# Nine input loads and three constants moved from the head of the filter stage's DMA queue to places between its stores

## The chip, the cores and the metric

One NeuronCore of one Trainium2 chip. The metric is the device time of one execution in microseconds, median of three runs.

## What is computed

One encoder layer over 2048 tokens of 1024 channels (batch 1). Cut to what matters here:

```
mod = silu(c) @ w_ada + b_ada ; shift, scale, gate = split(mod, 3)
u = x * (1 + scale) + shift
proj = u @ w_in + b_in                       # 1024 -> 3072 channels, all 2048 tokens
h = sin(...) of position features            # small network, three layers
k = (h @ w_out_filter) * decay ; k_freq = rfft([k forward, k backward], n = 4096)   # two filters x 512 channels
z = v ; for o, g in (x1, x2): z = g * (irfft(rfft(z) * k_freq[o]) + bias[o] * z)
y = concat(z * silu(gate_h), pooled branch * silu(gate_p))
out = LayerNorm(alpha * x + gate * (y @ w_out + b_out)) * ln_g + ln_b
```

## The kernel before, in words

The Fourier transforms are done as two stages of matrix products with a trip through HBM between them. Every fp32 product is three products of split operands (a "high" part, written by ScalarE, and a "low" part, the rest, written by VectorE). The program is a row of blocks with an all-engine barrier between some of them:

1. `front`: the small network, and the sums for `scale1` and `shift`. Its SP queue ends with the store of two gate rows (L357).
2. `filter_stage1` (scope `fs1`, L490 to L610): the filters are generated and go through the first transform stage. This is the stage that is changed.
3. `values_and_filters` (scope `p1`): the rest of the filters' transform, the forming and splitting of `u`, and the first tiles of the input projection.
4. Four more blocks, of the same kind as to queues, up to the output.

`filter_stage1` has N = 32 units, numbered n, two for each of 16 token groups m. For each unit:

- TensorE `gen(n)`: six matmuls into `gen_ps` (L538; the first two units have two more, L541).
- VectorE `window(n)`: times the decay, into `fs_k` (L570).
- ScalarE `high(n)`: `fs_khi` (L593). VectorE `low(n)`, one unit behind its window: `fs_klo` (L578).
- TensorE `stage1(n)`, three units behind `gen`: twelve matmuls into `s1_ps` (L554), with a table of 256 KB for each two units. The tables are loaded ahead on the GpSimd queue into a ring of three (L291).
- ScalarE `evac(n)`, three units behind `high`: copies `s1_ps` into one of three 512 KB buffers `xo[n % 3]` (L598). It waits for `stored[n % 3]`, that is, until the store of unit n - 3 has landed.
- SP: waits for `evac(n)` and stores the buffer to `kseq` in HBM, 512 KB (L516).

ScalarE takes its work in the order high(n), step(n - 2), evac(n - 3); `step` is empty but for unit 29, where it splits the first projection weight (`w_high(0)`, L761). VectorE ends the stage with `w_low(0)` and `form_u` of input pieces 0 to 3 (L720). TensorE runs gen(n), then stage1(n - 3); `stage1(n)` waits for `evac(n - 2)`.

The three `xo` buffers lie in memory that the projection owns and uses later (two thirds of `row`, half of `cv`); the eight buffers of `load_x` are `xin_xt` (two), `side`, the other half of `cv`, and `xin_pair` (four). Which piece goes to which:

```
def load_x(self, sp, m):
    tc, k2 = m // 4, m % 4
    src = self.t["t_xt"].rearrange("(k p) c -> p k c", p=P)
    after(sp, self.ulo_done[m % 8], m // 8)
    sp.dma_start(self.xt[m % 8][:, :, :], src[:, 2 * k2:2 * k2 + 2, tc * CH:(tc + 1) * CH]).then_inc(self.xt_in[m % 8], 16)
```

A piece is 512 KB in runs of 2 KB. Pieces 0 to 3 are first read by `form_u` at the end of the stage, pieces 4 to 7 in the next block. `load_w(sp, 0)` (L754) is 512 KB, first read by `w_high(0)`. `load_consts` (L746 to L748) are three small transfers, 38, 32 and 64 KB, first read in the next block.

Of the kernel before, what the change touches and what calls it, by code (L numbers as in the profile page):

```python
# [487 lines left out]
def group_rows(seq, g):  # L488

    return seq.rearrange("(p m g) c -> p g m c", m=2, g=GS)[:, g, :, :]  # L490


def filter_stage1(nc, t, tabs, fl, kseq, pj, owner):


    with Scope(nc, "fs1", cleared_with=owner) as s:
# [9 lines left out]
        N = 2 * GS  # L506

        @block.sync
        def _(sp):
            for m in range(8):  # L510
                pj.load_x(sp, m)
            pj.load_w(sp, 0)
            pj.load_consts(sp)
            for n in range(N):
                sp.wait_ge(evac_done[n % 2], n // 2 + 1)
                sp.dma_start(group_rows(kseq[n % 2], fl.group(n // 2)), xo[n % 3]).then_inc(stored[n % 3], 16)  # L516
            sp.wait_ge(fl.rows_out, 16)

        @block.gpsimd
# [1885 lines left out]
```

## Time and profile before

| | |
|---|---|
| median of 3 runs | 1191.55 us (1189.43 to 1192.32) |
| the profiled execution | 1192.32 us, span 1190.4 us |
| TensorE busy, share of the span | 92% |
| VectorE, ScalarE, GpSimd | 72%, 48%, 1% |
| HBM traffic | 273.24 MB, mean 230 GB/s |
| granted TensorE clock, mean | 0.971 of full |

The span is 1.9 us shorter than the execution's own time, since it begins with the first recorded instruction and ends with the last. Start times in the profile count from the span's start. Busy shares are means over stages with different limits, so the stage that is changed has to be read by itself: `filter_stage1` lies at 55 to 140 us.

### The profile page before, as it was taken

What the parts mean: (1) busy time and instruction counts of PE and PEld (TensorE: products, weight loads), DVE (VectorE), ACT (ScalarE), POOL (GpSimd) and SP (SyncE); (2) the same over time, 40 slices, a digit from 0 to 9 for tenths busy, and PEclk for the clock granted to TensorE, in tenths of its full rate; (3) what the DMA queues carried; (4) which work ended last, traced back from release to release, by engine and by line L of the source; (5) the groups of instructions that cost most, each with busy time, mean ns of one, the idle gap of its engine ahead of it and who ended that gap; (6) DMA issues with size and microseconds to landing.
All of it is one profiled execution on the core that took longest, in us unless ns stands there. A gap on an engine that the chain in (4) does not pass through costs nothing. (4 is left out here: it accounts for less than half of the span.)

```text
span 1190.4 us, 14193 instructions
## 1 busy us (share of the span) xinstructions
PE 1089.8 (92%) x4928; PEld 840.9 (71%) x4928; DVE 856.6 (72%) x1093; ACT 576.8 (48%) x757; POOL 12.6 (1%) x32
## 2 busy tenths in 40 slices
PE   3799789999999999989999998897999578999995
PEld 1278667888888777767888776665788467888883
DVE  6699976555454546559999555655999857888878
ACT  4078864434545344537777443442877753222210
POOL 0001000000000000000000000000000000000000
PEclk8789999999999999999999999999999889999998
DMA  9998845677674536688998578778899999557321
GB/s 338 350 310 285 288 164 162 195 249 248 217 254 161 176 109 213 229 253 240 275 297 258 160 235 268 232 254 212 245 298 261 306 308 311 156 184 211 125 89 54
DMA packets 155133, 273.24 MB, mean 230 GB/s; under 512 B 11504, under 2 KB 49520, under 8 KB 153397
## 3 DMA queue, kind: packets, MB, share of 16 engines
q1 hardware_dynamic: 151605, 266.74, 70.2%
q0 software_dynamic: 3168, 5.51, 2.0%
q8 instruction: 40, 0.66, 0.3%
q14 instruction: 32, 0.25, 0.1%
q10 hardware_dynamic: 288, 0.08, 0.0%
HBM read 178.95 MB, written 98.57 MB: 233 GB/s over the span
## 5 line engine op out<-in xcount | busy, mean ns | idle before, releaser
L177 PE MATMUL u_pp<-uh_uhi,prj_whi 128*128 128x512 f32 x768 | 310.3, 404 | 14.6 <-DVE u_ulo L741 9.1
L178 PE MATMUL u_pp<-u_ulo,prj_whi 128*128 128x512 f32 x768 | 305.2, 397 | 0.0
L179 PE MATMUL u_pp<-uh_uhi,prj_wlo 128*128 128x512 f32 x768 | 305.0, 397 | 0.0
L177 PEld LDWEIGHTS u_pp<-uh_uhi,prj_whi 128*128 128x128 f32 x768 | 146.0, 190 | 57.9 <-issue 14.9
L179 PEld LDWEIGHTS u_pp<-uh_uhi,prj_wlo 128*128 128x128 f32 x768 | 146.1, 190 | 34.6
L178 PEld LDWEIGHTS u_pp<-u_ulo,prj_whi 128*128 128x128 f32 x768 | 146.5, 191 | 32.3
L1256 DVE TENSOR_TENSOR p_alo<-xin_pair,p_ahi 128x1024 fp32r<-128x1024 f32 x32 | 39.2, 1226 | 100.8 <-ACT p_ahi L1193 100.8
L1193 ACT ACTIVATE p_ahi<-xin_pair 128x1024 fp32r<-128x1024 f32 x32 | 33.9, 1061 | 126.8 <-PE p_ps L179 119.0
L2195 ACT ACTIVATE p_sm<-p_mv,p_eps 128x1 f32<-128x1 f32 x16 | 4.7, 295 | 107.8 <-DVE p_mv L2286 107.8
L177 PE MATMUL p_first<-uh_uhi,prj_whi 128*128 128x512 f32 x128 | 51.5, 403 | 4.0 <-DVE p_y L2280 2.6
L593 ACT ACTIVATE fs_khi<-fs_k 128x1024 fp32r<-128x1024 f32 x32 | 34.0, 1061 | 41.2 <-DVE fs_k L570 41.2
L554 PE MATMUL fs_s<-fs_khi,flt_tab 64*128 64x512 f32 x256 | 50.1, 413 | 3.3 <-ACT prj_row L598 3.3
L1595 ACT ACTIVATE p_us<-p_u 64x512 f32<-64x512 f32 x64 | 38.1, 596 | 27.7 <-DVE p_y L1672 26.6
L178 PE MATMUL p_first<-uh_uhi,prj_whi 128*128 128x512 f32 x128 | 51.1, 399 | 0.0
L179 PE MATMUL p_first<-uh_uhi,prj_wlo 128*128 128x512 f32 x128 | 51.0, 399 | 0.0
L177 PE MATMUL p_b<-uh_uhi,prj_whi 128*128 128x512 f32 x128 | 50.6, 395 | 0.2 <-DVE p_us L2280 0.2
L179 PE MATMUL p_b<-uh_uhi,prj_wlo 128*128 128x512 f32 x128 | 50.5, 395 | 0.0
L178 PE MATMUL p_b<-uh_uhi,prj_whi 128*128 128x512 f32 x128 | 50.5, 395 | 0.0
L1678 DVE TENSOR_TENSOR p_us<-p_us,p_k_im 128x512 f32<-128x512 f32 x64 | 43.4, 688 | 9.4 <-ACT p_us L1596 6.2
L797 ACT ACTIVATE prj_row<-u_pp,prj_own 128x512 f32<-128x512 f32 x64 | 43.9, 687 | 6.6 <-PE u_pp L179 5.7
L900 ACT ACTIVATE prj_side<-u_pp,prj_own 128x512 f32<-128x512 f32 x32 | 38.9, 1216 | 13.2 <-PE u_pp L179 7.5
L570 DVE TENSOR_TENSOR fs_k<-fs_gen,flt_dec 128x1024 f32<-128x1024 f32 x32 | 38.8, 1212 | 7.7 <-PE fs_gen L541 7.7
(210 smaller groups left out, 2108.0 us busy)
## 6 DMA issues: line engine op xcount, KB each, us to landing
xin_pair<-kseq SPq DMA_DIRECT2D x32, 512.0 KB, 4.4
kfreq<-xin_pair SPq DMA_DIRECT2D x32, 512.0 KB, 5.2
xseq<-p_xo SPq DMA_DIRECT2D x32, 512.0 KB, 7.5
p_k_re<-kfreq SPq DMA_DIRECT2D x64, 256.0 KB, 5.5
p_k_im<-kfreq SPq DMA_DIRECT2D x64, 256.0 KB, 4.8
bseq<-p_out SPq DMA_DIRECT2D x32, 512.0 KB, 5.3
prj_ws<-in_t_win SPq DMA_DIRECT2D x24, 512.0 KB
kseq<-prj_row SPq DMA_DIRECT2D x22, 512.0 KB, 4.3
```

The costliest lines, as they stand in the source:

```text
L177: nc.tensor.matmul(out, w[0], m[0], start=start, stop=False, skip_group_check=True)
L178: nc.tensor.matmul(out, w[0], m[1], start=False, stop=False, skip_group_check=True)
L179: return nc.tensor.matmul(out, w[1], m[0], start=False, stop=stop, skip_group_check=True)
L554: mm = nc.tensor.matmul(s1_ps[r][:, jj, :], fl.tab[m % 3][js, h, a, :], k[r3][js, h, :], start=h == 0 and part == 0, stop=h == 1 and part ...
L570: nc.vector.tensor_tensor(kf[r3][:, :, :], gen_ps[n % 2][:, :, :], fl.dec[:, m // 2, :, :], ALU.mult).then_inc(k_done[r3], 1)
L593: nc.scalar.activation(khi[r3][:, :, :], kf[r3][:, :, :], ACT.Copy).then_inc(hi_done[r3], 1)
L797: self.nc.scalar.activation(self.row[:, PAD + c * CH:PAD + (c + 1) * CH], self.pp[q % 2][:, :], ACT.Identity, bias=self.b_in[:, col:col + ...
L900: self.nc.scalar.activation(by_group(self.sg[:, c % 2, :]), by_token(self.pj.pp[q % 2][:, :]), ACT.Silu, bias=self.pj.b_in[:, col:col + 1] ...
L1193: nc.scalar.activation(ahi[:, :, :], a[n % 2][:, :, :], ACT.Copy).then_inc(hi_done, 1)
L1256: nc.vector.tensor_tensor(alo[:, :, :], a[n % 2][:, :, :], f32(ahi[:, :, :]), ALU.subtract).then_inc(lo_done, 1)
L1595: nc.scalar.activation(us[0:64, i, :], u_ps[64:128, i, :], ACT.Copy, scale=-1.0)
L1678: nc.vector.tensor_tensor(us[:, i, :], us[:, i, :], k_im[:, i, :], ALU.mult).then_inc(turn_done, 1)
```

## The change

The nine loads and the constants are taken from the head of the SP queue of `filter_stage1` and issued behind stores of late units: the weight behind the store of unit 18, pieces 0 to 3 behind those of units 19 to 22, the constants behind unit 23, pieces 4 to 7 behind units 24 to 27. Nothing else differs: same transfers, same sizes, same buffers, same waits.

```diff
@@ -507,13 +507,17 @@
         @block.sync
         def _(sp):
-            for m in range(8):
-                pj.load_x(sp, m)
-            pj.load_w(sp, 0)
-            pj.load_consts(sp)
             for n in range(N):
                 sp.wait_ge(evac_done[n % 2], n // 2 + 1)
                 sp.dma_start(group_rows(kseq[n % 2], fl.group(n // 2)), xo[n % 3]).then_inc(stored[n % 3], 16)
+                if n == N - 14:
+                    pj.load_w(sp, 0)
+                if N - 13 <= n < N - 9:
+                    pj.load_x(sp, n - (N - 13))
+                if n == N - 9:
+                    pj.load_consts(sp)
+                if N - 8 <= n < N - 4:
+                    pj.load_x(sp, n - (N - 12))
             sp.wait_ge(fl.rows_out, 16)
```

## Rows read from the trace of the kernel before

**Rows 1.** Busy time by stretch; last three columns: TensorE clock, DMA share, GB/s.

```profile
core 0: us, PE busy (x) PEld busy (x) DVE busy (x) ACT busy (x) POOL busy (x), PEclk, DMA share, GB/s
55.00:70.00 15.00, 14.57 (x62) 8.49 (x64) 8.54 (x8) 4.69 (x5) 0.00 (x0) 0.59 1.01 373
70.00:80.00 10.00, 9.99 (x81) 7.86 (x79) 10.00 (x10) 8.54 (x10) 1.59 (x3) 1.00 0.78 259
...
120.00:130.00 10.00, 10.00 (x88) 8.93 (x86) 10.00 (x10) 8.83 (x10) 1.07 (x2) 1.00 0.95 315
```

**Rows 2.** Same view, stretches of 2 us: loads alone, then stores and tables.

```profile
66.00:68.00 2.00, 2.00 (x16) 1.62 (x14) 2.00 (x3) 1.06 (x1) 0.00 (x0) 0.70 1.05 396
...
70.00:72.00 2.00, 1.99 (x18) 1.50 (x16) 2.00 (x3) 1.71 (x3) 0.54 (x1) 1.00 0.34 45
78.00:80.00 2.00, 2.00 (x19) 1.61 (x17) 2.00 (x3) 1.71 (x3) 0.53 (x1) 1.00 1.05 408
```

**Rows 3.** ScalarE's timeline: start, duration, what; in brackets its idle time before.

```profile
70.74 1.06 ACT L593 ACTIVATE fs_khi<-fs_k 128x1024 fp32r<-128x1024 f32 x1 [0.29 <-DVE fs_k L570]
71.71 1.01 ACT L598 ACTIVATE prj_row<-fs_s 128x1024 f32<-128x1024 f32 x1
...
130.65 1.00 ACT L598 ACTIVATE prj_row<-fs_s 128x1024 f32<-128x1024 f32 x1
...
133.85 1.00 ACT L598 ACTIVATE prj_row<-fs_s 128x1024 f32<-128x1024 f32 x1
...
138.10 1.03 ACT L598 ACTIVATE prj_row<-fs_s 128x1024 f32<-128x1024 f32 x1 [0.38 <-PE fs_s L554]
```

**Rows 4.** Timeline of the SP queue, 69 to 140 us; x2 rows hold two stores.

```profile
70.48 2.82 SPq L516 DMA_DIRECT2D kseq<-prj_row  x2
...
111.27 2.78 SPq L516 DMA_DIRECT2D kseq<-prj_row  x2
...
137.75 1.91 SPq L516 DMA_DIRECT2D kseq<-prj_row  x2
```

**Rows 5.** Issue to landing of the 32 stores (L516), then of the store at 137.75 alone.

```profile
DMA to landing us min/median/max: 3.1/4.3/6.4
```

```profile
DMA to landing us min/median/max: 3.1/3.1/3.1
```

**Rows 6.** Waits from 70 to 140 us: who for whom, total, times, longest.

```profile
ACT prj_row L598 <- DMA kseq<-prj_row: 1.1, 2, 0.6
```

**Rows 7.** DMA queues, 100 to 130 us: q1 the stores, q0 the tables.

```profile
q1 hardware_dynamic: 3677, 7.08, 65.1%
q0 software_dynamic: 982, 1.78, 24.6%
```

**Rows 8.** The same view, 55 to 70 us, where the nine loads run.

```profile
DMA packets 2889, 5.59 MB, mean 373 GB/s; under 512 B 441, under 2 KB 537, under 8 KB 2886
```

**Rows 9.** The same view, 860 to 910 us: other loads and stores, engines full.

```profile
DMA packets 7537, 14.14 MB, mean 283 GB/s; under 512 B 658, under 2 KB 658, under 8 KB 7533
```

**Rows 10.** GpSimd's timeline: the last table loads.

```profile
111.10 0.53 POOL L291 DMA_DIRECT2D flt_tab<-in_t_w1f  x1 [4.01 <-PE fs_s L554]
...
125.06 0.53 POOL L291 DMA_DIRECT2D flt_tab<-in_t_w1f  x1 [3.66 <-PE fs_s L554]
```

**Rows 11.** Timeline of all engines, 52 to 80 us: the stage's first work.

```profile
55.43 1.65 PE L538 MATMUL fs_gen<-flt_wfil,flt_hfil 64*128 64x512 f32 x6 [3.07 <-PEq L250]
57.01 2.07 PE L541 MATMUL fs_gen<-flt_bias,flt_e 1*128 1x512 f32 x2
59.12 1.23 DVE L570 TENSOR_TENSOR fs_k<-fs_gen,flt_dec 128x1024 f32<-128x1024 f32 x1 [5.36 <-PE fs_gen L541]
...
62.69 1.23 DVE L570 TENSOR_TENSOR fs_k<-fs_gen,flt_dec 128x1024 f32<-128x1024 f32 x1 [2.35 <-PE fs_gen L541]
```

**Rows 12.** Timeline, 126 to 176 us: the next block's first work.

```profile
140.34 2.00 ACT L734 ACTIVATE uh_uhi<-xin_xt 128x1024 fp32r<-128x1024 f32 x2 [1.21 <-PEq L247]
```

**Rows 13.** DMA queues, 78 to 90 us: GB/s in 40 equal slices.

```profile
GB/s 396 410 423 396 410 410 416 219 61 0 55 68 246 417 389 396 430 403 403 403 423 410 212 109 212 27 27 328 369 389 382 375 396 403 382 396 382 150 68 102
```

## The prediction

> **What bounds the kernel now.** I read the slices of the page first, only to find the stage; then the stretches, for which engine is full in it; then ScalarE's timeline, for how much room each unit has; then the DMA rows, for what a transfer costs the sixteen engines; last the two ends of the stage. From 70 to 130 us VectorE is busy without a gap, and TensorE is too, nearly [rows 1]. Stores go out every 2.27 us: the one at 70.48 is unit 0, the one at 111.27 is unit 18, and (111.27 - 70.48) / 18 = 2.266 [rows 4]. That is VectorE's pace, two operations a unit. The thing to see is the DMA share beside it: 0.78 to 0.95 with the stores and tables alone [rows 1]. The stage is bound by VectorE, with the DMA engines close behind. The nine loads run from 55 to 70 us, where the share is 1.01 and nothing is stored yet [rows 1], since the first store is issued at 70.48 [rows 4]. They cost nothing there, as far as the rows show.
>
> **What a transfer costs the engines.** In 100 to 130 us the queue of the stores moved 7.08 MB in 65.1% of 30 us, which is 363 GB/s of engine time: a store of 0.524 MB takes 1.44 us. The tables moved 1.78 MB in 24.6%: one of 0.262 MB takes 1.09 us, one every two units [rows 7]. So a unit asks 1.44 + 0.54 = 1.98 of its 2.27 us, and 0.29 us is free. A load: 396 GB/s at a share of 1.05 [rows 2], about 390 over the whole of 60 to 68 us, hence 1.34 us. The constants are 0.134 MB in short packets. By bytes they take 0.35 us; 441 short packets at the stretch's mean of 15 x 16 / 2889 = 0.083 us over 16 engines take 2.3 us [rows 8]. I take 1.2.
>
> **The change, part by part.**
>
> *Taken from the head.* SP issued twelve transfers before its first store but the store waited for ScalarE anyway. VectorE's first two windows wait for TensorE [rows 11], which runs at the lower clock there (0.50 to 0.59 of full, that is 1.2 GHz for most of it) [rows 1]; none waits for a transfer. I take 0. From above the gain is bounded in the third rival.
>
> *Put in between.* From unit 18 to 27 each unit but one gets a load of 1.34 us into 0.29 us of room. That is 9 x 1.34 + 1.2 = 13.3 us of work into ten units with 2.9 us to spare, so the queue falls some 10 us behind. SP's own issuing does not matter: 0.51 us for the store and about 0.4 for the load in 2.27.
>
> *Who waits.* I take the queue to be served in order, so a store stands behind the load of the unit before. ScalarE's evac(n) may start only when store n - 3 has landed. Evacs are 2.27 us apart and the store goes out 1.0 us after its evac began, so a store may take 3 x 2.266 - 1.03 = 5.8 us. The median takes 4.3, the longest 6.4 [rows 5], and two of the 29 waits are already felt, 1.1 us together [rows 6]. These two cost VectorE nothing: behind a late evac stands the next high, which has 0.29 us of room [rows 3], and VectorE comes to low(n) one unit, 2.27 us, after window(n), of which the high takes 1.06 and its start 0.1: 1.1 left. So a delay of an evac up to about 1.4 us is swallowed, and beyond it VectorE, and TensorE through `stage1(n)`, are late too. The tables have their own queue and four units, 9 us, from issue to first use.
>
> *The sum.* The last wait of the kind is evac(31), which needs store 28. Store 18 is issued at 111.27 [rows 4]. A store alone lands 3.1 us after issue [rows 5], of which 1.44 is moving and 1.7 is not. From there the engines have no pause until store 28 is through: 11 stores (18 to 28) 15.8 us, 9 loads 12.1, the constants 1.2, and 4 tables (at 111.10 to 125.06) 4.4 [rows 10]: 33.5 us. Store 28 lands at 111.27 + 1.7 + 33.5 = 146.5. Before, evac(31) began at 138.10 [rows 3], so it is 8.4 us late. The same sum for store 25 (8 stores, 6 loads, constants, 4 tables: 25.1) gives 138.1, against evac(28) at 133.85, 4.2 late [rows 3]; for store 24 135.3, against evac(27) at 130.65, 4.7 late with its table counted. High(31) and `w_high(0)` stand behind that evac, so VectorE's last work is some 4 us late, and ends near 143, before 146.5. So store 28 ends last, and the whole 8.4 us reach the next block, which begins about 1.2 us after the last evac's end [rows 3, 12]. Its engines all start from a barrier, so nothing there gives it back. Its first needs, pieces 4 to 7, stood in the queue ahead of store 28 and have landed.
>
> The sum is 1192.32 + 8.4 = 1200.7 us against the profiled execution, which lies 0.8 above the median of 1191.55. For the median I say 1200.0.
>
> *Bounds.* The total is 11.67 MB (11 stores, 9 loads, 0.13 MB, 1.05 MB). At 408 GB/s, the best 2 us of stores and tables [rows 2], it takes 28.6 us: 3.5 us late. At 283 GB/s, the rate of another full stretch of loads and stores together [rows 9], 41.2 us: 16 us late. I take the middle, since it uses the durations of these very transfers; the stretch of rows 9 has shorter rows of other tensors.
>
> The Trainium skill, page "DMA: Bandwidth & Descriptors", section "Rules for kernel authors", says to issue a DMA early and wait on its semaphore late so that its cost overlaps compute, which speaks against this change. By that, the kernel before is the better one, and the trace agrees so far as the loads ran where no store was waiting.
>
> **Rivals.**
>
> *The queue is faster than its shares say.* A share counts time in which a packet waits as busy, so full may not be full. For it: among the stores single slices of 0.3 us reach 410 to 430 GB/s [rows 13]. Against it: 2 us of loads with nothing else go at 396 [rows 2]. If all ran at 430, 27.1 us: store 28 at 140.1, 2.0 us late, 1193.5. That is within what can be told from no change. The Trainium skill, same page, section "Anatomy of one DMA", fits 2.0 us plus bytes over 436 GB/s; an estimate from it is 28.8 us from issue, 1.9 us late. Its 3.2 us for a store of this size agrees with the 3.1 of the lone store [rows 5]; the tables' 241 GB/s [rows 7] do not fit it.
>
> *Loads and stores disturb each other.* No row of this stage shows both at once. If reading and writing HBM together goes as in rows 9, the stage loses up to 16 us: 1208. For it: that stretch and several like it are full at 283 to 306 GB/s. Against it: its transfers differ.
>
> *The head was held back by the loads.* The six matmuls of `gen(0)` take 1.65 us and the next two 2.07 [rows 11]. If this were the loads' doing and not the clock's, with half of it gone the first window would start 1.8 us sooner, the second would follow at 2.27 instead of 3.57: 3.1 us gained, up to 3.8 if the pair at L541 shrank further. With the later loads costing nothing at the same time, 1188.5. It decides only if the late loads lose less than this gains; for it speaks the share of 1.01 at the head [rows 1], against it that the granted clock there is the lower level, which explains the doubled durations by itself. A change that does nothing at all is the case of both sides at 0 and counted with the first rival.
>
> **How the numbers follow.** A measurement of this kernel tells about 0.3%, 3.6 us, from no change. The forecast, 4 to 13 us late, 0.66. Disturbed beyond that, up to 16 us, 0.12. Fast queue or hidden, less than 3.6 us, 0.18. Head gained, 0.04. Of the forecast's own low end a little falls to "same" already counted there. So slower 0.78, same 0.18, faster 0.04. The range is 1193 to 1206: it leaves out the lower half of the fast-queue case with the faster one, about 0.13, and 0.07 above.
>
> **What the changed profile would show.** ScalarE's `prj_row` and `prj_cv` (L598) waiting for DMA `kseq` at seven units or more, 10 us or more in all, instead of two waits and 1.1 us [rows 6]. Stores between 118 and 140 us landing 8 us or more after issue. DMA share at 1.0 from 112 to 145 us at 340 to 360 GB/s; a rate over 400 would be the first rival, under 310 the second. A share far below 1 in 56 to 70 us and the first windows still at 59.1 and 62.7; sooner is the third rival. VectorE gaps only from about unit 26 on. The first `uh_uhi` at about 148.7 instead of 140.34 [rows 12], and every later stage shifted by that. The prediction is wrong if the loads land as fast between the stores as at the head and no evac waits, or if the queue is not taken in order, so that a store passes a load.

## The result and the profile after

| | before | after |
|---|---|---|
| median | 1190.61 us (6 runs) | 1199.28 us (6 runs, 1195.09 to 1205.41) |
| ratio | | 1.0067, 95% interval 1.0043 to 1.0092 |
| span of the profiled execution | 1190.4 us | 1200.7 us |

The change makes the kernel slower by 0.67%, 8.0 us, with 5.1 to 11.0 us as its interval. The forecast was 8.4 us, in a range of 1193 to 1206 us.

The changed stage first, as busy time by stretch of the kernel after; the last three columns are TensorE's granted clock, the DMA share and GB/s.

```profile
core 0: us, PE busy (x) PEld busy (x) DVE busy (x) ACT busy (x) POOL busy (x), PEclk, DMA share, GB/s
55.00:70.00 15.00, 11.94 (x39) 6.25 (x41) 6.65 (x8) 2.66 (x3) 0.00 (x0) 0.50 0.10 40
...
120.00:130.00 10.00, 7.39 (x56) 5.81 (x54) 8.75 (x9) 6.30 (x7) 0.54 (x1) 0.93 1.07 371
130.00:140.00 10.00, 9.03 (x66) 7.31 (x66) 7.72 (x7) 7.61 (x8) 0.53 (x1) 0.90 1.06 380
140.00:150.00 10.00, 4.55 (x36) 3.07 (x32) 6.02 (x10) 5.29 (x6) 0.00 (x0) 0.96 1.00 384
```

The DMA share is the mean busy share of the core's sixteen DMA engines. At the head of the stage, where it was 1.01 before [rows 1], it now stands at 0.10, and from 120 us the DMA engines are full: 1.07, 1.06 and 1.00, at 371 to 384 GB/s. VectorE, at 10.00 of 10 before [rows 1], falls to 8.75 and 7.72.

ScalarE's timeline of the kernel after shows who waits (start, duration, in brackets the idle time before and its releaser):

```profile
123.12 1.03 ACT L602 ACTIVATE prj_row<-fs_s 128x1024 f32<-128x1024 f32 x1 [0.46 <-DMA kseq<-prj_row]
...
127.60 1.02 ACT L602 ACTIVATE prj_cv<-fs_s 128x1024 f32<-128x1024 f32 x1 [2.51 <-DMA kseq<-prj_cv]
...
130.81 1.03 ACT L602 ACTIVATE prj_row<-fs_s 128x1024 f32<-128x1024 f32 x1 [1.24 <-DMA kseq<-prj_row]
...
138.39 1.02 ACT L602 ACTIVATE prj_row<-fs_s 128x1024 f32<-128x1024 f32 x1 [0.45 <-DMA kseq<-prj_row]
...
141.20 1.01 ACT L602 ACTIVATE prj_row<-fs_s 128x1024 f32<-128x1024 f32 x1
143.66 1.03 ACT L602 ACTIVATE prj_cv<-fs_s 128x1024 f32<-128x1024 f32 x1 [1.45 <-DMA kseq<-prj_cv]
146.17 1.02 ACT L602 ACTIVATE prj_row<-fs_s 128x1024 f32<-128x1024 f32 x1 [1.48 <-DMA kseq<-prj_row]
148.72 1.02 ACT L602 ACTIVATE prj_row<-fs_s 128x1024 f32<-128x1024 f32 x1 [1.52 <-DMA kseq<-prj_row]
150.96 2.00 ACT L738 ACTIVATE uh_uhi<-xin_xt 128x1024 fp32r<-128x1024 f32 x2 [1.21 <-PEq L247]
```

From evac(22), at 123.12, nine of the ten evacs wait for a store three units back; evac(28), at 141.20, does not. The last three are 2.5 us apart, each released by a landing: a store and a load, one after the other, set their pace. The last of them began at 138.10 before, released by TensorE [rows 3]; now a landing releases it. The view of waits of the kernel after, 55 to 150 us, has the sum (two waits and 1.1 us before [rows 6], nine and 10.3 now):

```profile
ACT prj_row L602 <- DMA kseq<-prj_row: 5.7, 6, 1.5
ACT prj_cv L602 <- DMA kseq<-prj_cv: 4.6, 3, 2.5
```

VectorE's timeline of the kernel after has its three gaps in the stage, 3.9 us, two behind ScalarE and one behind TensorE:

```profile
129.60 1.23 DVE L582 TENSOR_TENSOR fs_klo<-fs_k,fs_khi 128x1024 fp32r<-128x1024 f32 x1 [1.25 <-ACT fs_khi L597]
132.68 1.23 DVE L574 TENSOR_TENSOR fs_k<-fs_gen,flt_dec 128x1024 f32<-128x1024 f32 x1 [1.85 <-PE fs_gen L542]
...
140.39 1.23 DVE L582 TENSOR_TENSOR fs_klo<-fs_k,fs_khi 128x1024 fp32r<-128x1024 f32 x1 [0.82 <-ACT fs_khi L597]
```

The gap of 1.85 us has a second cause beside the late evacs. TensorE stood idle for 2.12 us behind evac(23), and then its granted clock was at the lower of its two levels, 1.2 GHz, for 3 us (columns as in the first table of stretches; the clock is the third from the end, 0.50):

```profile
124.00:126.00 2.00, 1.71 (x14) 1.59 (x16) 2.00 (x2) 1.09 (x2) 0.00 (x0) 1.00 1.05 388
126.00:128.50 2.50, 0.64 (x6) 0.20 (x2) 2.36 (x3) 0.90 (x1) 0.00 (x0) 1.00 1.08 405
129.00:132.00 3.00, 3.00 (x16) 2.54 (x18) 1.23 (x1) 1.76 (x3) 0.01 (x1) 0.50 1.06 402
132.50:134.00 1.50, 1.50 (x16) 1.43 (x14) 1.32 (x2) 0.97 (x2) 0.02 (x1) 1.00 1.08 359
```

The matmuls of one unit, from the first of `stage1` to the end of `gen`, took 3.87 us there (128.77 to 132.64) where the unit before took 2.35 (124.29 to 126.64). With the 2.35 the gap would be 0.3 us, so about 1.5 us of it are the clock's.

One trap lies in these times. The next block begins 10.62 us later than before (150.96 against 140.34 [rows 12]), more than the whole loss. Part of it is there before the stage begins:

```profile
62.35 1.23 DVE L574 TENSOR_TENSOR fs_k<-fs_gen,flt_dec 128x1024 f32<-128x1024 f32 x1 [5.35 <-PE fs_gen L545]
65.93 1.23 DVE L574 TENSOR_TENSOR fs_k<-fs_gen,flt_dec 128x1024 f32<-128x1024 f32 x1 [2.35 <-PE fs_gen L545]
```

The first window starts at 62.35 against 59.12 [rows 11]. So I measure the stage by itself, from the start of the first window to the start of the last evac: 138.10 - 59.12 = 78.98 us before, 148.72 - 62.35 = 86.37 after, 7.39 us more. From the next block's first `uh_uhi` to the end of the span there are 1050.1 us before and 1049.7 after; in a second execution of each (e1 and e2 below) 1047.0 and 1047.2. So in neither pair is anything given back later, though this stretch too differs by 3 us between executions of one kernel.

### The profile page after: what moved, and what is told of

It is laid out like the page before. It is cut to its first block and busy times, and to the rows that moved or that the text cites. A ratio compares the mean times of both kernels' runs of the same rounds, so it can differ in the third digit from the quotient of the medians.

```text
span 1200.7 us, 14193 instructions
## 1 busy us (share of the span) xinstructions
PE 1099.5 (92%) x4928; PEld 846.2 (70%) x4928; DVE 857.5 (71%) x1093; ACT 577.2 (48%) x757; POOL 12.6 (1%) x32
## 5 line engine op out<-in xcount | busy, mean ns | idle before, releaser
L178 PEld LDWEIGHTS u_pp<-u_ulo,prj_whi 128*128 128x128 f32 x768 | 147.0, 191 | 32.8
```

The lines of the kernel that those rows point to most:

```text
L178: nc.tensor.matmul(out, w[0], m[1], start=False, stop=False, skip_group_check=True)
```

## The experiments

All stage lengths are from first window to last evac, in the profiled execution of each kernel. The ratio is to the kernel before on the same chip, for those kernels that have several executions (six of the change, ten of each other); e1, e2, e9, e10 and e11 are one execution each.

| kernel | first window | last evac | stage | late by | ratio, 95% interval |
|---|---|---|---|---|---|
| before | 59.12 | 138.10 | 78.98 | | |
| e1 before, again | 62.40 | 141.40 | 79.00 | 0.0 | |
| after | 62.35 | 148.72 | 86.37 | 7.4 | 1.0067 (1.0043 to 1.0092) |
| e2 after, again | 59.79 | 145.50 | 85.71 | 6.7 | |
| e3 halves | 59.72 | 141.30 | 81.58 | 2.6 | 1.0048 (1.0024 to 1.0071) |
| e4 four buffers | 58.68 | 141.57 | 82.89 | 3.9 | 1.0048 (1.0028 to 1.0068) |
| e5 spread | 59.55 | 142.62 | 83.07 | 4.1 | 1.0027 (0.9998 to 1.0055) |
| e6 last four | 59.97 | 144.72 | 84.75 | 5.8 | 1.0040 (1.0016 to 1.0065) |
| e7 ScalarE's queue | 60.98 | 147.57 | 86.59 | 7.6 | 1.0059 (1.0034 to 1.0084) |
| e8 first five | 60.32 | 143.19 | 82.87 | 3.9 | 1.0041 (1.0018 to 1.0063) |
| e9 last four, again | 60.19 | 142.46 | 82.27 | 3.3 | |
| e10 two apart | 62.41 | 141.62 | 79.21 | 0.2 | |
| e11 behind the last | 60.26 | 139.27 | 79.01 | 0.0 | |

### Is the late start part of the change? (e1, e2)

Neither kernel has an edit; each is one more execution. What was expected:

> The kernel before, once more. In the two profiles so far the block before the changed stage ended 3.2 us later after the change than before it (first window at 62.35 against 59.12), which the diff does not touch. Theory: that is variation between executions, so the first window here can start anywhere from 58 to 63, while the stage itself, from the start of the first window to the start of the last evac, is 79.0 us again, within 0.3. Rival: the late start belongs to the change, and the first window is at 59.1 again within 0.3.

> The changed kernel once more. Theory: the first window varies as in the kernel before, and the stage from first window to last evac is 86.4 us again within 0.7. Rival, the late start belongs to the change: first window at 62.4 within 0.3.

VectorE's timeline of e1, the kernel before:

```profile
62.40 1.23 DVE L570 TENSOR_TENSOR fs_k<-fs_gen,flt_dec 128x1024 f32<-128x1024 f32 x1 [5.37 <-PE fs_gen L541]
```

The kernel before starts its stage at 62.40 this time, and the changed one at 59.79. The start belongs to the execution, not to the change; the stage itself repeats to 0.02 us before and to 0.7 us after. In e2 TensorE's granted clock stays at 1.00 from 120 to 140 us, and VectorE's gaps come to 2.9 us instead of 3.9. Where two profiles are compared, the varying part ahead of the change has to be taken off first.

### Does the amount matter, or the place? (e3, e5)

```diff
+            for m in range(8):
+                pj.load_half(sp, m, 0)                       # e3: first halves at the head
             for n in range(N):
...
-                    pj.load_x(sp, n - (N - 13))
+                    pj.load_half(sp, n - (N - 13), 1)        # and the second halves where the change has the piece
...
-                    pj.load_x(sp, n - (N - 12))
+                    pj.load_half(sp, n - (N - 12), 1)
```

> Each of the eight pieces is loaded as two transfers of 256 KB, the first half of all at the head of the queue, the second half where the change puts the piece; weight and constants as in the change. Theory, the DMA engines are full and the loss is their surplus of work: 5.4 us less between the stores, so the sum gives 3.0 us late instead of 8.4, and with the 1.0 us by which the sum was high, 2 to 3 us: stage 81 to 82. Rival, the loss comes from there being a transfer behind each store (issue, order), whatever its size: 7.4 us, stage 86.4.

Measured: 81.58, 2.6 us late, inside 81 to 82. As many transfers stand behind the same stores as in the change, and taking 2.1 of their 4.85 MB away takes away nearly two thirds of the loss. So it is the work, not the issue.

```diff
-                if n == N - 14: ...                          # e5: all four places of the change
+                if n == 0:
+                    pj.load_w(sp, 0)
+                if n == 1:
+                    pj.load_consts(sp)
+                if n % 3 == 0 and 3 <= n < 27:
+                    pj.load_x(sp, n // 3 - 1)
```

> All nine loads still between stores, but spread: the weight behind unit 0, the constants behind unit 1, a piece behind units 3, 6, 9 and so on to 24. Theory, surplus of work per unit: three units ask 3 x 1.98 + 1.34 = 7.28 us of 6.80, so the backlog grows by 0.5 us per load to some 5.5 us at unit 25; 2.9 us of it is swallowed, so the stage is 1.5 to 3 us late: 80.5 to 82 us from first window to last evac. Rival, a load between stores costs the same wherever it stands: 7 us, stage 86.

Measured: 83.07, 4.1 us late, over the 1.5 to 3 expected and far from 7. Spreading helps as it should, but the sum was too low. Its VectorE timeline has most of it at an unexpected place, in the first half of the stage:

```profile
90.72 1.23 DVE L580 TENSOR_TENSOR fs_klo<-fs_k,fs_khi 128x1024 fp32r<-128x1024 f32 x1 [1.26 <-ACT fs_khi L595]
93.03 1.23 DVE L572 TENSOR_TENSOR fs_k<-fs_gen,flt_dec 128x1024 f32<-128x1024 f32 x1 [1.09 <-PE fs_gen L540]
95.94 1.23 DVE L572 TENSOR_TENSOR fs_k<-fs_gen,flt_dec 128x1024 f32<-128x1024 f32 x1 [0.55 <-PE fs_gen L540]
```

That is 2.9 us of gaps around unit 11, where by the terms of the sum the backlog was at most 2.7 us (the weight, the constants and one piece, 3.9, less four units' 0.29) and should have been swallowed. Two things add to it. The first is in the landing of store 4, issued at 80.33: the last of its sixteen landing events comes at 88.6, 2.5 us after their median, and evac(7) waits 2.32 us for it; e6 shows this more clearly. The second is TensorE's clock. TensorE stood idle for 1.85 us behind that evac, and then its granted clock fell to the lower level, 0.50:

```profile
88.00:90.00 2.00, 0.15 (x4) 0.15 (x4) 1.46 (x2) 1.29 (x2) 0.00 (x0) 1.00 1.05 351
90.00:91.00 1.00, 1.00 (x10) 0.94 (x12) 0.28 (x1) 1.00 (x2) 0.00 (x0) 1.00 0.75 285
91.50:94.00 2.50, 2.50 (x14) 2.31 (x12) 1.41 (x2) 2.07 (x3) 0.53 (x1) 0.50 0.84 299
```

The two units that it touches took 3.1 and 3.2 us from the first matmul of `stage1` to the end of `gen`, instead of 2.35. The two later gaps, 1.09 and 0.55 us, stand behind these matmuls.

### Is it the buffer that evac waits for? (e4)

```diff
-        xo, stored = pj.k_out, pj.k_stored
+        xo, stored = pj.k_out + [s.sb("xo3", [P, 2, DH])[:, :, :]], pj.k_stored
...
-                after(act, stored[n % 3], 16 * (n // 3))
+                after(act, stored[n % 4], 16 * (n // 4))
```

(the store, the semaphores and their waits in the next block go from three to four likewise)

> The changed kernel with a fourth buffer for evac, so that evac(n) waits for store n - 4 instead of n - 3. Theory, the loss is evac waiting for its buffer while the engines are full: the last evac then waits for store 27, which has one store and one load (2.8 us) less ahead of it: 4.6 to 5.6 us late, stage 83.6 to 84.6, and VectorE without gaps or with less than 1 us of them. Rival, what is late is something else (the tables, TensorE's clock, the final barrier): 7.4 us, as before.

Measured: 82.89, 3.9 us late instead of 7.4 and 6.7. In this execution the same transfers at the same places cost about half with one more buffer, as they should if the wait for the buffer carries the loss. How much of the gain holds for the kernel is less sure: the profiled execution was the fastest of e4's ten (1191.31 us, median 1197.49), and the interval of its ratio overlaps that of the change. My expectation was 0.7 too high at its lower end. One gap of VectorE is left, 1.49 us, over the 1 us expected. Its last evac still waits for a landing:

```profile
141.57 1.02 ACT L602 ACTIVATE fs_xo<-fs_s 128x1024 f32<-128x1024 f32 x1 [1.55 <-DMA kseq<-fs_xo]
```

### Is it the order within one queue? (e7)

```diff
                 nc.scalar.activation(xo[n % 3], s1_ps[n % 2][:, :, :], ACT.Copy).then_inc(evac_done[n % 2], 1)
+                if n == N - 14:
+                    pj.load_w(act, 0)
+                if N - 13 <= n < N - 9:
+                    pj.load_x(act, n - (N - 13))
...
```

> All nine loads and the constants at the same units as in the change, but issued on ScalarE's queue behind evac(n). Theory, the sixteen engines are full whatever the queue: 6 to 7.4 us late, stage 85 to 86.4. Rival, the harm is that a store stands behind a load in one queue and is taken in order: a store then shares the engines with at most one load, and the stage is at most 3 us late, 82.

Measured: 86.59, 7.6 us late, as with one queue (0.2 above the expected band). The rival's 3 us falls: another issuing engine does not help when the sixteen engines themselves are full (1.05 and 1.04 from 120 to 140 us). TensorE's clock stays at 1.00 over these 20 us, so a loss of this size needs no lower clock. The edit changes more than the queue, though. ScalarE's queue issues each load as its evac starts (the evac at 120.14, its load at 120.16), so the load goes out a microsecond ahead of the same unit's store (121.19) and not behind it; and issuing the three constants holds the next `high` back by 0.53 us. The last two evacs are released by TensorE here, not by a landing, so the loss does not come by quite the same path.

### Which of the loads? (e6, e8, e9)

```diff
-            for m in range(8):                               # e6, e9
+            for m in range(4):
                 pj.load_x(sp, m)
             pj.load_w(sp, 0)
             pj.load_consts(sp)
             for n in range(N):
...
+                if N - 8 <= n < N - 4:
+                    pj.load_x(sp, n - (N - 12))
```

> Only pieces 4 to 7 between stores (units 24 to 27), the rest at the head. Theory: from store 24 (nominally 124.87) to store 28 there are 5 stores, 4 loads and a table, 13.6 us, store 28 lands at 140.2, 2.1 us after the last evac's time before; with the error seen in the other sums 1 to 2.1 us: stage 80 to 81.1, VectorE without a gap. Rival, these last four make the loss, since only they stand ahead of the last stores: over 5 us, stage 84 or more.

Measured: 84.75, 5.8 us late. This is a miss, and the rival's number. VectorE has no gap, as I expected; ScalarE's timeline has four of its five waits for a store at the very end:

```profile
137.04 1.02 ACT L600 ACTIVATE prj_row<-fs_s 128x1024 f32<-128x1024 f32 x1 [2.22 <-DMA kseq<-prj_row]
139.59 1.02 ACT L600 ACTIVATE prj_cv<-fs_s 128x1024 f32<-128x1024 f32 x1 [1.52 <-DMA kseq<-prj_cv]
142.15 1.02 ACT L600 ACTIVATE prj_row<-fs_s 128x1024 f32<-128x1024 f32 x1 [1.54 <-DMA kseq<-prj_row]
144.72 1.02 ACT L600 ACTIVATE prj_row<-fs_s 128x1024 f32<-128x1024 f32 x1 [1.55 <-DMA kseq<-prj_row]
```

The trace has sixteen landing events for each of these transfers, one for each DMA engine, and the semaphore is full with the last. Sorted, in us, for three transfers of e6:

```
store 24   129.9 130.0 130.0 130.0 130.0 130.1 130.1 130.1 130.1 130.1 130.1 130.2 130.2 130.2 130.2 130.3
piece 4    131.1 131.2 131.2 131.2 131.2 131.4 131.4 131.5 131.5 131.5 131.6 131.6 131.7 132.9 133.8 135.6
store 28   140.9 141.0 141.0 141.0 141.0 141.0 141.0 141.0 141.1 141.1 141.1 141.3 141.4 141.9 142.8 144.6
```

Thirteen engines have store 28 by 141.4. The sum said 140.2 for the stage's nominal place, and with the 0.85 by which this stage starts later, 141.05. So it was right for nearly all the engines. One comes 3.6 us after the median, and evac(31) waits for that one, with a store's landing at 144.6 and its start at 144.72. The lag arises between store 24, where all sixteen stand within 0.5 us, and piece 4, where it is 4 us; from there to store 28 it hardly shrinks. My reading is that an engine that always has work waiting cannot catch up. Single packets of that time hint at what holds an engine: two of 2 KB that took 1438 and 1075 ns at 131.1 and 131.2 where the median is 84, and at 132.82 an instruction fetch of 16 KB, 951 ns. That these packets were on the lagging engine is inferred; the trace does not give a packet's engine.

If that is so, the loss of the same kernel must vary with the lag. Hence e9, the same kernel once more:

> The kernel of e6_last_four once more. There the stage was 5.8 us late where the sum gave 2.1, and the landing events of store 28, one for each of the sixteen engines, show why: twelve engines had it at 141.0 to 141.3, where the sum put it (140.2 and 0.85 for the later start of the stage), the slowest at 144.6. New theory: a transfer lands with its slowest engine, one engine is held up now and then for 1 to 4 us (an instruction fetch of 16 KB, a slow packet), and where the engines are full it does not catch up. Then the lag of the slowest engine, and the stage with it, differ from run to run: stage 79 + 2 + that lag (0.5 to 4 us), the lag read from the landing of store 28, and the median engine again within 0.7 of the sum. Rival: loads just ahead of the last stores simply cost more: stage 84.7 again within 0.5, with all sixteen engines late alike.

Measured: 82.27, 3.3 us late. Its landing events of store 28:

```
store 28   140.3 140.4 140.4 140.4 140.6 141.1 141.3 141.4 141.4 141.4 141.4 141.4 141.5 141.6 141.7 142.4
```

The stage starts 1.07 us later than before, so the sum says 141.3; the median engine has it at 141.4, the slowest at 142.4, a lag of 1.0 where e6 had 3.6. The sum 2.1, the lag 1.0, and 0.1 to 0.2 of rounding and from landing to start make the 3.3. The rival said 84.7 again, all engines alike. It falls, on one further execution.

```diff
+            for m in range(4, 8):                            # e8: pieces 4 to 7 to the head, the rest as in the change
+                pj.load_x(sp, m)
             for n in range(N):
...
-                if N - 8 <= n < N - 4:
-                    pj.load_x(sp, n - (N - 12))
```

> Only the weight, pieces 0 to 3 and the constants between stores (units 18 to 23); pieces 4 to 7 at the head. Theory: the backlog of these alone makes VectorE late once, by the 1.6 to 3.1 us of gaps that the two profiles of the change show before pieces 4 to 7 can matter, and the last evacs follow VectorE: 2 to 3 us late, stage 81 to 82. With the last four alone at 1 to 2.1 the two parts sum to less than the 6.7 to 7.4 of the change, as each part swallows its own first 2.9 us. Rival, no swallowing: the parts are each in proportion to their work, 4 and 3.4 us.

Measured: 82.87, 3.9 us late, above the expected 2 to 3 and at the rival's 4 for this part. With e9's 3.3 and e6's 5.8 the two parts sum to 7.2 and 9.7, not less than the whole. So my claim that each part swallows its own first 2.9 us is wrong for these two. Store 28, the last that an evac waits for, shows why. In the kernel before, store 28 is issued at 134.88, after evac(28), and has landed at 137.96, 3.07 us later; evac(31) starts at 138.10. The evac can be late because the store is issued late or because it lands slowly. The issue times, counted from the first window of each run, and the landing events tell the two apart (late and slower against the kernel before, in us):

| kernel | store 28 issued late by | landing slower by | sum | stage late by |
|---|---|---|---|---|
| after | 4.1 | 3.3 | 7.5 | 7.4 |
| e2 after, again | 3.6 | 3.2 | 6.8 | 6.7 |
| e8 first five | 3.9 | 0.0 | 3.9 | 3.9 |
| e9 last four, again | 0.0 | 3.3 | 3.4 | 3.3 |
| e6 last four | 2.4 | 3.5 | 5.8 | 5.8 |

The first five loads make the late issue, by way of late evacs, VectorE and TensorE; the last four, which stand just ahead of store 28, make the slow landing. The latter has no room at all: store 28 lands 0.1 us before its evac in the kernel before. So the two parts add. In e6 the lag of the slowest engine makes store 25 late as well, 2.2 us at evac(28), and that is nearly all its difference from e9.

### Is there room at all? (e10)

```diff
-            for m in range(8):
+            for m in range(6):
                 pj.load_x(sp, m)
...
+                if n == 12:
+                    pj.load_x(sp, 6)
+                if n == 20:
+                    pj.load_x(sp, 7)
```

> Only pieces 6 and 7 between stores, behind units 12 and 20; the rest at the head. Theory: 1.34 us of backlog is under the 1.5 us that a store may be late before an evac waits, and is worked off in five units of 0.29 us each; an evac may wait some tenths, VectorE has no gap and the stage stays at 79.0, within 0.3. Rival, every load between the stores costs its share, 7.4 / 9 = 0.8 us: stage 80.6.

Measured: 79.21. ScalarE's timeline of e10 has two late evacs:

```profile
88.98 1.03 ACT L602 ACTIVATE prj_row<-fs_s 128x1024 f32<-128x1024 f32 x1 [0.27 <-DMA kseq<-prj_row]
...
110.23 1.02 ACT L602 ACTIVATE prj_row<-fs_s 128x1024 f32<-128x1024 f32 x1 [1.12 <-DMA kseq<-prj_row]
```

The first comes before either load is issued, like those of the kernel before. The second, evac(16) at 110.23, waits 1.12 us for store 13, behind the first load. VectorE has one gap, of 0.12 us: it is swallowed. The second load leaves no mark. Two loads far apart are nearly free (0.2 us); nine close together cost 7.

### Where would they be free of the stores? (e11)

```diff
+                if n == N - 1:
+                    for m in range(4, 8):
+                        pj.load_x(sp, m)
```

(pieces 0 to 3, the weight and the constants at the head)

> Pieces 4 to 7 behind the last store (unit 31), the rest at the head. Theory: no store stands behind a load, so the stage up to its last evac is 79.0 within 0.3. But SP must issue four more transfers of about 0.5 us before it comes to the end of the block, so the next block's first uh_uhi stands 83.1 us after the first window instead of 81.2 (before) and 88.6 (after). Rival, the late pieces are missed in the next block: form_u waits for DMA there by 2 us or more.

Measured: stage 79.01. The next block, on ScalarE's timeline of e11:

```profile
139.27 1.02 ACT L601 ACTIVATE prj_row<-fs_s 128x1024 f32<-128x1024 f32 x1 [0.37 <-PE fs_s L557]
144.03 2.00 ACT L737 ACTIVATE uh_uhi<-xin_xt 128x1024 fp32r<-128x1024 f32 x2 [3.74 <-PEq L247]
```

It begins 144.03 - 60.26 = 83.8 us after the first window, where 83.1 was expected and 81.2 is the figure before: SP's issuing (2.68 us for the four) stands ahead of the barrier. The waits for late pieces in the next block are 0.5 and 0.3 us, so the rival falls. The execution took 1199.8 us, though, 7.6 more than the one run beside it, and only 2.5 us of it are explained here; from `uh_uhi` to the end there are 1054.0 us against 1050.1 and 1047.0 in the two executions before, and at most 1052.2 in any other run here. With one execution, that stays open. (The single executions of e9 and e10 were 1.8 and 2.8 us above the same run.)

## Why the prediction was right, point by point

*Taken from the head, 0.* Right. The first two windows are 3.58 us apart after, 3.57 before [rows 11], with the DMA share at 0.10 instead of 1.01 and the lower TensorE clock (0.50) in both; the six and the two matmuls of the first unit take 1.65 and 2.07 us with the loads beside them and without. The rival that the loads held the head back is dead: they were free there.

*Evacs wait; VectorE is late second.* Right in the main: nine waits and 10.3 us (seven and 10 or more were forecast), VectorE late by 3.9 us in all (some 4). With the 3.23 us of the late start taken off, evac(27), at 138.39, is 4.5 us late (4.7 forecast), and evac(28), at 141.20, 4.1 (4.2). Some of this agreement is luck: evac(28) waited for no landing (that of store 25 came 0.2 us before it), and about 1.5 us of VectorE's 3.9 came by TensorE's lower clock, of which the prediction's path has no term.

*The queue falls some 10 us behind.* Wrong as put, and without effect on the sum. No store of the kernel after lands later than 9.4 us after issue:

```profile
DMA to landing us min/median/max: 3.5/4.7/9.4
```

The three stores issued at 119.06 to 124.17 take 8.5 to 9.4 us, the next 7.2, and those from 131.86 to 142.24 only 6.4 to 6.7, where the prediction wanted 8 or more throughout. The queue cannot fall further behind, since an evac that waits for store n - 3 holds back the issue of its own store: the surplus turns into late evacs instead of into a longer queue.

*Store 28 ends last.* Right, shown by the releaser of the last evac, and supported by e4: with one more buffer the same loads cost 3.9 us in its profiled execution.

*The sum, 8.4 us.* Measured 7.4 and 6.7 for the stage, 8.0 for the kernel (5.1 to 11.0). Errors stood against each other, and that the forecast came so near is in part luck. The work of 33.5 us took less: the landing events of store 28 after give 147.4 for the median engine, which is 32.8 us after store 18's issue at 114.52, less the 1.7 fixed 31.1 us. A share of full engines reads 1.05, not 1.00 (1.07 and 1.06 above), and 33.5 / 1.05 is 31.9. Most of the rest is the constants' term: their 384 packets took 0.52 us of the sixteen engines, not 1.2, since the 441 short packets of [rows 8] hold 216 of 4 bytes that are no data of theirs, and short packets take 9 to 27 ns, not the mean of 83. And a term was missing: the slowest engine has store 28 at 148.6, 1.3 us after the median. -2.4 and +1.3 are -1.1, and 8.4 - 1.1 is 7.3. In e2 the same two are -2.9 and +1.2, which gives the 6.7 there.

*The bounds.* 408 GB/s and 283 GB/s around the measured 371 to 384: the choice of the transfers' own durations was right, but the reason for setting the far stretch aside was not. Its rows are no shorter: 6873 of its 7537 packets have 2 KB, like these. Why it goes at 283 no run here shows. The first rival (fast queue, 430) is dead at 371 to 384, though its premise, that full is not quite full, was worth the 5% above; so is the second: loads and stores together went nearly as fast as the 396 GB/s of the loads alone [rows 2]. The forecast of 340 to 360 GB/s was too low by the same 5%.

*Nothing given back.* Right within each pair: 1049.7 against 1050.1 us, 1047.2 against 1047.0.

*Its own tests.* `uh_uhi` was to come 8.4 us later than before; of the 10.62 found, 3.23 are the late start, which e1 shows in the kernel before too. VectorE's gaps were to begin at about unit 26; the first is at `low(27)`.

The Trainium skill's rule named in the prediction (page "DMA: Bandwidth & Descriptors", section "Rules for kernel authors": issue a DMA early, wait on its semaphore late) agrees with the result; both orders wait late, and the one that issues early costs 8.0 us less. The page's reason is the fixed setup cost, which this way overlaps with compute; what was lost here is the engines' time between the stores. Its fit of section "Anatomy of one DMA", which it gives for a single DMA issued from GpSimd, gave 1.9 us late for this change, by 436 GB/s throughout; the 371 to 384 GB/s measured and the 7.4 us decide against using it for this mix.

What stays open: what holds single packets for over a microsecond, how much of the loss TensorE's lower clock makes in the kernel after (in e2 it stayed high, and the stage was 0.7 us shorter), and whether e3 and e4 cost more than their stages show. Their ratios are 5.7 us each, where the one profiled stage was 2.6 and 3.9 us late; the interval of e4 holds its figure (3.3 to 8.1), that of e3 begins just above it (2.9 to 8.5). The lag of the slowest engine, which differs between executions, could make this, but I have it for the profiled ones alone.

## What to carry to other kernels

Before moving a transfer, add up what the DMA engines have to do per unit of the loop around its new place, from the durations of the same transfers in the trace: here 1.98 of 2.27 us, so that each load of 1.34 us at the new place was mostly surplus, while at the old place nothing else moved. A surplus costs nothing until it is more than the buffers' tolerance, and all of it after that; just ahead of the last store there is no tolerance, and all of it counts. A further buffer halved the cost in the one execution profiled, another issuing queue did not help. And compare stages by their own length, since what lies ahead of them varies by 3 us from one execution to the next, and what lies behind them too.

## What the runs showed of the hardware that I had not expected

A transfer has landed when the slowest of sixteen engines has, and the engines do not stay together. With room, they meet again within about three units: before, 2.1 us at stores 6 and 7, 0.3 at store 9. With full engines a lag of 1 to 4.2 us is carried from transfer to transfer (in e6 4.2 us at store 25 and 3.6 still at store 28). The head of the stage before has it too: 3.0 us at the first piece and 2.8 at the eighth. It costs the kernel before little: of the store issued at 84.07 fifteen engines land by 88.5 and one at 90.4, after an instruction fetch of 16 KB that took 2296 ns at 85.21, and this is one of the two evacs that wait there [rows 6].

```
store 6, before   88.0 88.0 88.3 88.3 88.3 88.3 88.3 88.3 88.3 88.4 88.4 88.4 88.4 88.4 88.5 90.4
```
